# All five score levels of a head in one visit to the tiled array of TensorE, with a new order of VectorE's work and a new opening, in a hybrid decoder layer

## What is computed

```python
b = jnp.cumsum(g_, axis=-2)
diff = b[..., :, None, :] - b[..., None, :, :]
decay = jnp.exp(jnp.where(causal, diff, -jnp.inf))
A = jnp.einsum('bhid,bhjd,bhijd->bhij', q_, k_, decay)
o_intra = jnp.einsum('bhij,bhje->bhie', A, v_)
```

## Time and profile before

| | |
|---|---|
| median of 3 runs | 877.41 us (877.16 to 878.36) |
| the profiled execution, its own time | 877.31 us |
| its span (first to last instruction) | 875.6 us |
| PE busy | 855.6 us (98%), 5379 instructions |
| DVE busy | 602.3 us (69%), 982 instructions |
| ACT busy | 413.1 us (47%), 554 instructions |
| granted clock of TensorE | 0.999; the page's PEclk row reads 9 in all 40 slices |
| DMA | 167.74 MB, mean 192 GB/s |

### The profile page before, as it was taken

The page is one execution under the profiler, slowest core; times in us unless marked ns, Lnnn a source line. Parts: engine busy times, 40 slices in busy tenths (PEclk is TensorE's granted clock), DMA queues, the critical chain, the costliest instruction groups (busy, mean ns, idle before and its releaser), DMA issues.

```text
span 875.6 us, 13716 instructions
## 1 busy us (share of the span) xinstructions
PE 855.6 (98%) x5379; PEld 698.8 (80%) x5379; DVE 602.3 (69%) x982; ACT 413.1 (47%) x554; POOL 85.1 (10%) x128
## 2 busy tenths in 40 slices
PE   8999999999999999999999999999999999999996
PEld 5886888888888878888778778778788888888885
DVE  5723377753587747577887888889885678556756
ACT  6621442324445325273464655745555455335454
POOL 4010111110000001011111100000111100000000
PEclk9999999999999999999999999999999999999999
DMA  7386569989755846567776655545776988865654
GB/s 263 96 276 217 168 186 236 202 193 242 237 173 154 276 145 202 166 181 162 165 156 149 140 176 160 164 131 181 153 159 136 289 201 268 309 203 181 202 172 192
DMA packets 75170, 167.74 MB, mean 192 GB/s; under 512 B 7333, under 2 KB 15561, under 8 KB 73961
## 3 DMA queue, kind: packets, MB, share of 16 engines
q1 hardware_dynamic: 45266, 108.02, 37.4%
q0 software_dynamic: 16896, 50.34, 26.8%
q10 hardware_dynamic: 12952, 8.61, 3.5%
HBM read 158.56 MB, written 58.72 MB: 248 GB/s over the span
## 4 chain that ended last, share of the span: by engine, by line
PE 72%; DVE 16%; ACT 5%; issue 3%; DMA 3%; DVEq 1%; ACTq 0%
PE main L554 42%; PE main L805 8%; PE main L747 5%; PE sc L805 4%; DMA raw<-in_w_in 3%; DVE w_lo L1237 3%; PE po L805 2%; PE st L805 2%; DVE att L1348 1%; ACT w_hi L847 1%; PE sc L612 1%; PE sc L747 1%; PE po L640 1%; PE po L643 1%; PE st L625 1%
## 5 line engine op out<-in xcount | busy, mean ns | idle before, releaser
L554 PE MATMUL main<-h_hi,w_hi 128*128 128x512 f32 x640 | 256.6, 401 | 0.1
L554 PE MATMUL main<-h_hi,w_lo 128*128 128x512 f32 x640 | 250.0, 391 | 0.0
L554 PE MATMUL main<-h_lo,w_hi 128*128 128x512 f32 x640 | 249.6, 390 | 0.0
L1237 DVE TENSOR_TENSOR w_lo<-raw,w_hi 128x1024 fp32r<-128x1024 f32 x102 | 124.6, 1222 | 118.0 <-ACT w_hi L847 117.1
L847 ACT ACTIVATE w_hi<-raw 128x1024 fp32r<-128x1024 f32 x102 | 107.8, 1058 | 192.4 <-PE main L554 134.7
L554 PEld LDWEIGHTS main<-h_hi,w_lo 128*128 128x128 f32 x640 | 120.1, 188 | 26.0
L554 PEld LDWEIGHTS main<-h_hi,w_hi 128*128 128x128 f32 x640 | 120.2, 188 | 25.6 <-issue 0.5
L554 PEld LDWEIGHTS main<-h_lo,w_hi 128*128 128x128 f32 x640 | 120.4, 188 | 23.1
L868 ACT ACTIVATE ex<-ex 128x512 f32<-128x512 f32 (+2 forms) x84 | 52.4, 641 | 59.1 <-DVE ex L1377 49.2
L554 PE MATMUL main<-w_hi,h_hi 128*128 128x512 f32 x128 | 50.5, 395 | 0.3 <-DVE val L1491 0.3
L1708 DVE TENSOR_TENSOR w_lo<-feat,w_hi 128x1024 fp32r<-128x1024 f32 x26 | 31.8, 1224 | 27.4 <-ACT w_hi L1161 27.2
(11 more groups left out here) (307 smaller groups left out, 1494.1 us busy)
## 6 DMA issues: line engine op xcount, KB each, us to landing
raw<-in_w_in SPq DMA_DIRECT2D x104, 512.0 KB, 4.6
w_sum<-in_w_out POOLq DMA_DIRECT2D x48, 512.0 KB, 5.0
w_sum<-in_w_in POOLq DMA_DIRECT2D x24, 512.0 KB, 6.0
w_sum<-w_sum POOLq DMA_DIRECT2D x24, 512.0 KB, 5.4
raw<-w_sum SPq DMA_DIRECT2D x24, 512.0 KB, 3.5
feat<-w_sum SPq DMA_DIRECT2D x24, 512.0 KB, 3.5
raw<-in_w_out SPq DMA_DIRECT2D x14, 512.0 KB, 4.6
feat<-in_x SPq DMA_DIRECT2D x6, 1024.0 KB, 7.4
```

What stands on the lines that cost most here:

```text
L554: mm = pe.matmul(main[c][:, :], a, b, start=(k == 0 and j == 0), stop=(k == KT - 1 and j == 2))
L1237: dve.tensor_tensor(w_lo[:, q % SPL, :, :], raw[:, q % RAW, :, :], w_hi[:, q % SPL, :, :], ALU.subtract).then_inc(lo_ok, 1)
```

## The change

Every level of a merged head now has operands and a place of its own, so that all five are multiplied in one visit, in slot 16 (`alone`) or 8 (`shared`, `hg_pair`). `level_at` gives the place: for the ten heads with `quads_in` = `po`, level 0 in `sc[0]`, 1 in `sc[1]`, 2 in `po`, 3 in the free columns of `sc[1]` and `po`, 4 in `st`, the bank of the states. The packed level therefore waits for the first states (`s_ok`), and the second state product of a GLA head for the last copy. `O` and partly `U` and `M` move one slot later. On VectorE the states and the scaling of levels 4 and 5 come before all five copies, the copies stand one step later, and `cut` stands before the next head's `early`; on ScalarE `take` stands before `early` in the HGRN pairs and at the end of the shared groups. In the opening the first tile comes in two transfers and is squared in two halves, its first half normalised in two quarters; the second half of the norm's weights comes by a broadcasting transfer instead of two products and ScalarE's copies; pieces 2 and 3 of the weights go to buffers of their own (`first_raw`) without a wait; and the last split of group 0 comes after the copies of the values.

```diff
-KL = [0, 1, 1, 2, 1]
+KL = [0, 1, 1, 2, 3]
...
+        def level_at(at, l, c):
+            if l == 0:
+                return sc[0], c * P
+            if l == 1 or l == 2:
+                return (sc[1] if l == 1 else at["quads_in"]), c % 2 * QW
+            if at["quads_in"] is sc[0]:
+                return (sc[1], c * P // 2) if l == 3 else (sc[0], c * P)
+            return ((sc[1], po)[c // 2], 2 * QW + c % 2 * P // 2) if l == 3 else (st, c * P)
...
-            x_tile(0)
+            for a in range(2):
+                h = slice(a * D // 2, (a + 1) * D // 2)
+                sp.dma_start(xin[:, 0, h], x[0:P, h]).then_inc((x_left, x_in[0])[a], 16)
             group(w_in, C_GV, G_V, range(0, 2))
+            sp.dma_start(nwb[:, D // 2:], norm_w[D // 2:].partition_broadcast(P)).then_inc(nb_in, 16)
...
-                        if l > 2 or l == 2 and into[l] is sc[0]:
+                        if l >= 2 and apart:
                             pe.wait_ge(sc_ok, H * NL + (l - 1))
+                        elif l == PACKED:
+                            pe.wait_ge(s_ok, X + 1)
...
+                        else:
+                            pe.wait_ge(sc_ok, H * NL + NL)
...
-            for j in range(4):
+            for j in range(2):
                 pe.matmul(main[j][:, :], ones[0:1, :], nrow[:, j * 512:(j + 1) * 512], start=True,
...
-            pe.wait_ge(nb_ok, 2)
-            filler(4)
+            filler(7)
...
-            alone = dict(T=7, L=[12, 12, 12, 16, 16], U=[13, 22], O=[19, 24], M=28)
-            shared = dict(T=0, L=[4, 4, 4, 8, 8], U=[3, 12], O=[11, 15], M=20)
+            alone = dict(T=7, L=[16] * NL, U=[13, 22], O=[19, 24], M=28)
+            shared = dict(T=0, L=[8] * NL, U=[4, 13], O=[12, 16], M=21)
             second = dict(T=17, L=[18, 21, 21, 25, 25], U=[20], O=[28], M=31)
-            earlier = alone | dict(U=[13, 20], O=[19, 22], M=26)
+            earlier = alone | dict(U=[13, 21], O=[20, 23], M=27)
+            alone |= dict(O=[20, 24])
...
-                    todo |= head_tasks(hg_at(m, u) | dict(T=z, L=[z + 4, z + 4, z + 4, z + 8, z + 8], U=[z + 3],
-                                                          O=[z + 11], M=z + 15 - u))
+                    todo |= head_tasks(hg_at(m, u) | dict(T=z, L=[z + 8] * NL, U=[z + 4], O=[z + 12], M=z + 15))
...
-                    todo[z + 2] = [f for x in nxt for f in (x["decay"], x["values"], x["early"])] + [h["take"](0)]
+                    todo[z + 2] = [f for x in nxt for f in (x["decay"], x["values"])] + [h["take"](0)] + [
+                        x["early"] for x in nxt]
...
-                    dve.wait_ge(sc_ps, H * NL + (l + 1))
+                    dve.wait_ge(sc_ps, H * NL + (4 if l in (1, 2) and quads_in is po else l + 1))
...
-                    todo[z + 1] = [cp(0), cp(1), cp(2), sl(4), h["states"](0), sl(5)]
-                    todo[z + 2] = ([x["args"] for x in nxt] + [cp(3), cp(4)]
-                                   + [f for x in nxt for f in (x["ends"], x["early"])] + [h["cut"]])
+                    todo[z + 1] = [h["states"](0), sl(4), sl(5)]
+                    todo[z + 2] = ([cp(0), cp(1), cp(2), cp(3), cp(4)] + [f for x in nxt for f in (x["args"], x["ends"])]
+                                   + [h["cut"]] + [x["early"] for x in nxt])
```

More of the change, by code:

```diff
@@ L389, in group @@
                     last = QP if isinstance(G, int) and G == G_C and p < RAW else RAW
-                    if not (isinstance(n, int) and n < RAW):
-                        sp.wait_ge(lo_ok, n - last + 1)
+                    if not (isinstance(n, int) and n < 2 * RAW):
+                        early = RAW if isinstance(n, int) and n < 3 * RAW else 0
+                        sp.wait_ge(lo_ok, n - last - early + 1)
                     rows = src[p * PK * P:(p + 1) * PK * P, bass.ds(col, GW)]
+                    if isinstance(n, int) and RAW <= n < 2 * RAW:
+                        sp.dma_start(first_raw[:, s, :, :], rows.rearrange("(k p) n -> p k n", p=P)).then_inc(
+                            first_in[s], 16)
+                        continue
                     sp.dma_start(raw[:, s, :, :], rows.rearrange("(k p) n -> p k n", p=P)).then_inc(raw_in[s], 16)
@@ L674, in transposes @@
             def transposes(t, half):
-                pe.wait_ge(xn_ok, 2 * t + half + 1)
                 for j in (2 * half, 2 * half + 1):
+                    if t == 0 and j == 0:
+                        pe.wait_ge(xq_ok, 1)
+                    else:
+                        pe.wait_ge(xn_ok, 2 * t + half + 1)
                     if t:
@@ L1236, in split, with group @@
                 dve.wait_ge(hi_ok, first_piece(G) + (q + 1))
-                dve.tensor_tensor(w_lo[:, q % SPL, :, :], raw[:, q % RAW, :, :], w_hi[:, q % SPL, :, :],
+                first = isinstance(G, int) and RAW <= G * NP + q < 2 * RAW
+                dve.tensor_tensor(w_lo[:, q % SPL, :, :], (first_raw if first else raw)[:, q % RAW, :, :],
+                                  w_hi[:, q % SPL, :, :],
                                   ALU.subtract).then_inc(lo_ok, 1)
-            def group(G, tasks, take, first=0):
+            def group(G, tasks, take, first=0, last=NP):
                 for p in range(NP):
-                    if p >= first:
+                    if first <= p < last:
                         split(G, p)
@@ L1248, in group @@
                     take(c)
+                for p in range(last, NP):
+                    split(G, p)
                 for f in tasks.get("end", ()):
@@ L1444, in _, with normalise @@
             dve.tensor_copy(ones_r[:, :], ones).then_inc(onesr_ok, 1)
-            def normalise(t, half):
-                h = slice(half * D // 2, (half + 1) * D // 2)
-                if half == 0:
+            def normalise(t, half, cols=slice(0, D // 2)):
+                h = slice(half * D // 2 + cols.start, half * D // 2 + cols.stop)
+                if half == 0 and cols.start == 0:
                     dve.wait_ge(xss, t + 1)
@@ L1465, in _ @@
             dve.wait_ge(nb_ok, 2)
-            normalise(0, 0)
+            normalise(0, 0, slice(0, 512))
+            normalise(0, 0, slice(512, D // 2))
             split(0, -3)
@@ L1492, in values @@
                 return f
-            group(0, {}, values(0), 1)
+            group(0, {}, values(0), 1, NP - 1)
             dve.wait_ge(par_ps, 1)
@@ L1626, in shared_steps @@
                 return {0: [g["quads"], ar(4), sl(3), ar(5)],
[L1627 to L1628 removed]
+                        1: [g["states"](0), sl(4), sl(5)],
+                        2: [cp(0), cp(1), cp(2), cp(3), cp(4), s["args"], s["ends"]], 3: [g["states"](1), s["early"], g["cut"]],
                         4: [s["quads"], ar2(4), cp2(0), sl2(3), ar2(5)],
[L1630 to L1631 removed]
+                        5: [cp2(1), cp2(2), sl2(4), sl2(5), s["states"](0), g["norm"]],
+                        6: [cp2(3), cp2(4), nxt["args"], nxt["ends"], s["cut"], nxt["early"]], "end": [s["norm"]]}
             group(G_C, gla_steps(0), lambda c: None)
```

105 lines of the change are left out of this document (60 added, 45 removed).

## The result

The changed kernel takes **885.97 us** (median of 4 runs, 885.44 to 886.84) where the kernel before takes 877.28 us (4 runs, 877.11 to 878.36): a ratio of 1.0096, 95% interval 1.0084 to 1.0108. It is slower by about 8.7 us; 874.0 was predicted, in a range of 870 to 878.5.

What follows compares the result with a forecast made beforehand. TensorE, busy 98% of the span, was taken as the bound. Terms -2.9 - 6.4 - 2.7 + 9.8 + 1.0 - 2.1 gave -3.3 us from 877.31: 874.0 us, range 870 to 878.5.

Steps and rivals of the forecast that it cites:

- One visit less: Score products of ten heads: merging two visits into one saves 0.29 us each, -2.9 us.
- the waits in the visit: Inside score visits: five TensorE waits for scaled queries vanish, 5.9 us and restarts, -6.4 us.
- the mean-square waits: Before the mean-square product: four waits vanish with `cut` ahead of `early`, 1.7 us and restarts, -2.7 us.
- the shared groups: Two groups where an HGRN head follows a GLA head: packed level and score products slightly late, +1.0 us.
- The gates: Two loop boundaries: VectorE reaches the next group's gates late, TensorE waits 4.9 us at each, +9.8 us.
- the gates come at V + 12.6, in time: Last head pair: no head follows, `early` is missing, so no wait for gates.
- At the start of the loop ScalarE empties the banks, and nothing waits.: Boundary into the loop, where ScalarE frees the banks: no TensorE wait, priced at nothing.
- The clock behind a gap, taken at nothing: Work behind the two gate gaps: the sum adds no loss for a slower TensorE clock.
- rival 1: Behind both gate gaps TensorE briefly runs at half speed, 1.5 us lost twice: 877.0 us; chance 17%.
- The opening: Kernel start: scale ready sooner, smaller first normalise, two broadcasts fewer, so transposes start earlier, -2.1 us.
- the 0.7 us for squaring in halves: Opening: squaring the row's first half before the second lands gives the scale 0.7 us sooner.
- second visit to second visit: Loop: from the second head's visit to the same in the next pass, 56.7 us before, about 58.7 predicted.

Runs made afterwards that it cites:

- (6): Changed kernel with the group ends rewoven on ScalarE and VectorE (split, exponentials, pieces of `early` moved), no work added or left out: 870.80 us, ratio 0.9916.
- experiment 1: Changed kernel with VectorE's `early` for the next group's head behind the four gates instead of ahead, in the loop: 882.16 us, ratio 1.0054.
- (8): Rewoven kernel with the second GLA head's inverse root behind the stores instead of ahead of them: 870.98 us, ratio 0.9923.
- experiment 5: Kernel before, two visits a head, with only the change's loop order (`take` before exponentials, `cut` before `early`): 884.85 us, ratio 1.0088.
- experiment 2: Changed kernel, merged visit kept, with the loop's old order (exponentials ahead of `take`, `early` ahead of `cut`): 890.61 us, ratio 1.0149.

## Why the prediction was wrong

The forecast of 874.0 us lies 12.0 us under the measurement. Two of its steps failed: it said that nothing waits where ScalarE empties the banks, which cost 4.1 us, and it took the clock behind a gap at nothing, which cost 6.0 us. Point by point:

- *One visit less, the waits in the visit, the mean-square waits* (-2.9, -6.4, -2.7, with +1.0 for the shared groups: -11.0). **Right.** Of the 10.29 us lost between the two milestones, 14.8 are waits at group starts and 6.0 the clock; the rest is 10.29 - 20.8 = -10.5 us. No wait stands in a visit or before a mean square. The pieces can be read from TensorE's timeline with the prediction's own method: the 20 visits of the ten heads cost 27.4 us, the ten merged ones 18.8, so 8.7 us less where 9.3 were forecast. A merged visit costs 1.74 to 1.89 us outside the loop (1.75 forecast) but 1.94 to 2.11 in it. The four late mean squares cost 0.93, 0.93, 1.34 and 1.42 us where one in time costs 0.47, together 2.7 us more, as forecast. In the shared groups no wait appears, and one group of output products in each costs 0.2 us more: 0.4 instead of the 1.0 forecast. That makes -11.0; the 0.5 us between it and the -10.5 is not placed. Merged visits with gates and stores out of the way (6) are worth 6 to 7.5 us net, with some 4.5 us of waits for gates, stores and a score copy still standing.
- *The gates* (+9.8). **Right in mechanism and size**, with V the start of the second head's visit: V + 18.7 for the first matmul against the 18.2 predicted, gaps of 4.99 and 4.75 us. The third gate wait, 0.92 us in the last pair, was missed ("the gates come at V + 12.6, in time"): ScalarE's SiLU was the later one. The cause was named too narrowly: VectorE's `early` was on the path, but taking its 4.87 us away shortened the gaps by only 2.0 and 1.8 us (experiment 1), because ScalarE's path was nearly as long; a chain of two engines has to be walked on both.
- *"At the start of the loop ScalarE empties the banks, and nothing waits."* **The first failed step: 4.1 us.** At the ends of groups 6 and 7 (0.60 and 2.03 us) the same order that put `take` ahead of the exponentials put 1.87 us of exponentials behind the score products, in front of the stores. In group 7 ScalarE's first store begins at 500.49, while TensorE's last matmul of the group begins at 498.80 and the next group's first, after 2.03 us of standing, at 501.23. With the split moved, and in group 7 two of the four exponentials put behind the stores, both waits are gone (6); the old order was not put back there by itself. At the end of group 5 (1.47 us) ScalarE's order is the old one: there its first store comes 1.75 us sooner than before (383.47 against 385.22), but TensorE, rid of its waits and with a visit less for each head, is ready 3.2 us sooner (384.22 - 1.47 = 382.75 against 385.96). The 1.3 us of the inverse root stand in front of these stores, and with it behind them the wait falls to 0.23 (8). I walked the gates' boundaries and not those where ScalarE alone frees the banks.
- *The clock behind a gap, taken at nothing.* **The second failed step, and the largest: 6.0 us.** It was rival 1 with 17%, priced at 1.5 us for each of two gaps, from a slow phase of about 3 us that the earlier trace rows leave open (slow transposes end at 12.66, fast ones begin at 18.37); the rows of the changed kernel say 1.6, 2.1 and 2.3 us for three gaps, because the one for the stores of group 7 had not been foreseen. The Trainium skill (TensorE: Matmul & The Clock Gate, section "HAM oscillation — how this bites in real kernels") says that an idle gap long enough drops the engine to half its clock and the work behind it starts slow; the trace agrees, with 0.50 granted from 562 to 566. The printed clock of the kernel before, 1.00 with no wait over 1.3 us in the body, says nothing against it, and I let it weigh.
- *The opening* (-2.1). **Too large by 0.6 to 1.2**: 1.47 us in the changed kernel's trace (1.1 over all traces), 0.9 us by itself. The failed term is the 0.7 us for squaring in halves, which was 0.1.

Missed waits 5.0 (4.1 and 0.9), clock 6.0, opening 0.6, visits 0.5: 12.1 us, the miss. Of what was to be seen in the profile, the pause before `cut` (1.69), the two long waits and the vanished ones came as written; second visit to second visit took 604.59 - 543.39 = 61.2 us instead of 58.7, of which the slow clock is 2.1; rows at twice the pitch said that the clock was the rival that held. One sign failed: the first main matmul came 0.85 us sooner (12.77 against 13.62), not 1.5 to 2.5.

## What to carry to other kernels

A gap on a busy TensorE can cost more than its length: behind 10 of the 13 gaps of 2 us or more in the table below, 1.3 to 2.3 us more were lost. Price every predicted wait of that size with the slow matmuls behind it, and if it can't be avoided, fill it. When work moves on one engine, walk every engine that has a hand in freeing the next buffer, at every boundary of the program and not only at the one that the change was written for. An order that lets one product start sooner (`cut` before `early`) pays only if what it pushes back isn't what the next group waits for; the pauses it leaves, and the time between one freed bank and the next, are where the pushed work fits.

## What the runs showed of the hardware

Whether the clock falls behind a gap isn't settled by the gap's length alone. Idle time before the first matmul of a group, and the time of its first 24 main matmuls (5.7 at full clock), in the change and eight kernels of the experiments, where a head's transposes stand in the stretch:

| idle, us | 24 matmuls, us |
|---|---|
| 0.97 to 1.49 (14 gaps) | 5.66 to 5.70 |
| 2.02 to 2.04 (5 gaps) | 7.27, 7.26, 7.27; 5.69, 5.67 |
| 2.95, 2.96 | 7.23, 6.99 |
| 3.28, 3.28 (same kernel, both passes) | 7.28, 5.67 |
| 4.99, 4.75, 4.99, 4.74 | 7.81, 8.01, 7.56, 7.93 |

The two gaps of 3.28 us in experiment 5, each with its first and 24th matmul:

```profile
562.66 0.50 PE L554 MATMUL main<-h_hi,w_hi 128*128 128x512 f32 x1 [3.28 <-DVE feat L1659]
...
569.94 0.39 PE L554 MATMUL main<-h_hi,w_lo 128*128 128x512 f32 x1
...
622.63 0.47 PE L554 MATMUL main<-h_hi,w_hi 128*128 128x512 f32 x1 [3.28 <-DVE feat L1659]
...
628.30 0.39 PE L554 MATMUL main<-h_hi,w_lo 128*128 128x512 f32 x1
```

The same instructions and the same gap, once at half clock and once not. None of the gaps of the table under 1.5 us was followed by a slow stretch, every one over 4.7 was, and between them both occurred. A short gap is no safeguard where another stands just ahead of it. In experiment 2, one of 0.60 us behind the mean square's 2.01 was followed by 24 matmuls in 8.00 us:

```profile
561.64 0.79 PE L677 MATMUL po<-lrw,ones_r 128*128 128x512 f32 x1 [2.01 <-DVE sq_lo L1466]
...
563.47 0.77 PE L576 MATMUL main<-h_hi,w_hi 128*128 128x512 f32 x1 [0.60 <-DVE feat L1704]
```

In the gaps of 4.99 and 4.75 us of the changed kernel the granted clock fell while TensorE stood; in that of 2.03 us it reads 0.94 from 500 to 502 and 0.50 from 502 to 504, with TensorE at work again since 501.23. What decides for gaps between 2 and 3.3 us was not tried and stays open.
